# The high halves of the weights written by a converting DMA from GpSimd, instead of by GpSimd additions

## What is computed

```python
# first block
h = rmsnorm(x, pre_norm_g)
q, k, v, g_a, u_p, g_p = split(h @ w_in)                      # 1024 x 2304
a = banded_attention(q, k, v, rel_bias, attn_sink) * silu(g_a)
p = multiscale_pool(u_p, pool_w, pool_scale) * silu(g_p)
x = x + rmsnorm(concat([a, p]) @ w_out, post_norm_g)
# second block
h = rms_norm(x, norm1_g)
q, k, v, bg, cg, xc = split(h @ w_in_2)                       # 1024 x 6144
y_attn = chunked_relpos_attention(q, k, v, q_norm_g, k_norm_g, rel_bias) @ w_attn_proj
y_conv = gated_short_conv(bg, cg, xc, conv_w, conv_b) @ w_conv_proj
g_attn, g_conv = split(sigmoid(h @ w_gate + b_gate))
x = x + (g_attn * y_attn + g_conv * y_conv) @ w_out
h2 = rms_norm(x, norm2_g)
x = x + square(relu(h2 @ w_up)) @ w_down                      # 1024 x 4096 x 1024
```

## Time and profile before

| | us |
|---|---|
| median of 3 runs | 2715.04 (2714.69 to 2716.16) |
| the profiled execution, its own time | 2712.78 |
| its span in the profile | 2710.9 |
| PE busy | 2378.0 (88%) |
| PE weight loads busy | 2121.8 (78%) |
| DVE busy | 1203.3 (44%) |
| POOL busy | 926.5 (34%) |
| ACT busy | 677.1 (25%) |
| read from HBM, written | 160.83 MB, 60.82 MB |

### The profile page before, as it was taken

The page is one execution under the profiler, slowest core; times in us unless marked ns, Lnnn a source line. Parts: engine busy times, 40 slices in busy tenths (PEclk is TensorE's granted clock), DMA queues, the critical chain, the costliest instruction groups (busy, mean ns, idle before and its releaser), DMA issues. The chain is left out here.

```text
span 2710.9 us, 38552 instructions
## 1 busy us (share of the span) xinstructions
PE 2378.0 (88%) x14666; PEld 2121.8 (78%) x14666; DVE 1203.3 (44%) x2564; ACT 677.1 (25%) x1341; POOL 926.5 (34%) x736
## 2 busy tenths in 40 slices
PE   6237887378799969999999998999999999999999
PEld 6236766277799968888888876888979989889889
DVE  5006767636356626666666656133332122131121
ACT  3005545313200015555555512121211010010110
POOL 3031220234344422222222235444244444354352
PEclk9668997588999989999999999999989999999999
DMA  7833321221222232323333245222111111111112
GB/s 150 118 81 81 92 66 52 98 109 70 86 78 85 86 110 79 91 81 87 94 94 90 79 160 209 94 93 101 48 32 59 46 37 47 48 47 48 48 47 79
DMA packets 217453, 223.55 MB, mean 82 GB/s; under 512 B 81592, under 2 KB 185560, under 8 KB 217320
## 3 DMA queue, kind: packets, MB, share of 16 engines
q1 hardware_dynamic: 103384, 128.23, 16.4%
q10 hardware_dynamic: 113936, 93.44, 11.5%
HBM read 160.83 MB, written 60.82 MB: 82 GB/s over the span
## 5 line engine op out<-in xcount | busy, mean ns | idle before, releaser
L139 POOL TENSOR_TENSOR w_hi<-w_raw,zero 128x512 fp32r<-128x512 f32 x356 | 412.8, 1190 | 1589.9 <-PE ps L184 1298.7
L184 PE MATMUL ps<-a_hi,w_hi 128*128 128x512 f32 x1600 | 580.7, 409 | 20.7 <-DVE a_lo L374 9.9
L184 PE MATMUL ps<-a_lo,w_hi 128*128 128x512 f32 x1600 | 558.9, 395 | 5.8 <-issue 5.8
L184 PE MATMUL ps<-a_hi,w_lo 128*128 128x512 f32 x1600 | 559.3, 395 | 0.0
L184 PE MATMUL ps<-w_hi,a_hi 128*128 128x256 f32 x1472 | 424.8, 289 | 102.2 <-PEq L603 88.4
L144 POOL TENSOR_TENSOR w_lo<-w_raw,w_hi 128x512 fp32r<-128x512 f32 x356 | 471.9, 1357 | 7.0
L184 PE MATMUL ps<-w_lo,a_hi 128*128 128x256 f32 x1472 | 422.1, 287 | 0.0
L184 PE MATMUL ps<-w_hi,a_lo 128*128 128x256 f32 x1472 | 421.7, 286 | 0.0
L184 PEld LDWEIGHTS ps<-w_hi,a_hi 128*128 128x128 f32 x1472 | 288.9, 196 | 104.0 <-POOL w_lo L144 83.2
L184 PEld LDWEIGHTS ps<-a_hi,w_hi 128*128 128x128 f32 x1600 | 304.6, 191 | 75.9 <-issue 22.1
L184 PEld LDWEIGHTS ps<-a_hi,w_lo 128*128 128x128 f32 x1600 | 304.3, 190 | 67.5
(11 more groups left out here) (138 smaller groups left out, 2789.6 us busy)
## 6 DMA issues: line engine op xcount, KB each, us to landing
w_raw<-in_w_in_dram SPq DMA_DIRECT2D x33, 1024.0 KB, 5.2
feat_fm<-stage_a ACTq DMA_DIRECT2D x64, 256.0 KB, 2.0
w_raw<-in_w_up_dram SPq DMA_DIRECT2D x16, 1024.0 KB, 5.5
w_raw<-in_w_down_dram SPq DMA_DIRECT2D x16, 1024.0 KB, 5.1
qk_raw_a<-qkv_tm ACTq DMA_DIRECT2D x48, 256.0 KB, 3.8
conv_in<-feat_fm ACTq DMA_DIRECT2D x24, 512.0 KB, 5.5
qkv_tm<-stage_tm ACTq DMA_DIRECT2D x11, 1024.0 KB, 5.2
res<-in_x_dram SPq DMA_DIRECT2D x16, 512.0 KB, 6.0
```

What stands on the lines that cost most here:

```text
L139: hi = nc.gpsimd.tensor_tensor(w_hi[slot][:, k:k + 2, :], w_raw[:, k:k + 2, :], zero[:, 0:1].unsqueeze(2).to_broadcast([P, 2, CW]), ALU.add)
L184: last = nc.tensor.matmul(out_of(o), lhs, rhs(o), start=first and n == 0, stop=final and n == 2)
```

## The change

The four additions of zero that made the high half are gone. In their place POOL issues, as soon as the slot is free, one DMA of 1 MB that reads the chunk again from HBM and writes it into `w_hi`; source float32 and destination fp32r differ, so the DMA converts. Then POOL waits for both `raw_in` and `hi_done` (16 for each DMA now) and makes the low half with the same four subtractions as before. `w_raw` is still loaded by SP, in the same order. `split_weights` now needs the address of the chunk and so walks over `segs`; `phase_mlp` has the same edit by hand. PE, DVE, ACT and SP keep their instructions.

```diff
-        def pieces(slot, high_ready):
-
-            for k in range(0, KB, 2):
-                hi = nc.gpsimd.tensor_tensor(w_hi[slot][:, k:k + 2, :], w_raw[:, k:k + 2, :],
-                                             zero[:, 0:1].unsqueeze(2).to_broadcast([P, 2, CW]), ALU.add)
-            hi.then_inc(hi_done, 1)
-            high_ready()
+        def low_parts(slot):
+
             for k in range(0, KB, 2):
                 lo = nc.gpsimd.tensor_tensor(w_lo[slot][:, k:k + 2, :], w_raw[:, k:k + 2, :],
                                              w_hi[slot][:, k:k + 2, :].bitcast(F32), ALU.subtract)
             lo.then_inc(split_done, 1)
 
+        def rounded(w, row0, col):
+
+            return w[row0, :].rearrange("(k p) n -> p k n", p=P)[:, :, col]
+
...
-            def one(n, slot):
-                pool.wait_ge(raw_in, (n + 1) * 16)
+            def one(n, slot, w, row0, c):
                 if not (isinstance(n, int) and n - 2 < start):
                     pool.wait_ge(*used(n - (2 + start)))
-                pieces(slot, lambda: pool.wait_ge(hi_done, n + 1))
...
+                pool.dma_start(w_hi[slot][:, :, :], rounded(w, row0, c)).then_inc(hi_done, 16)
+                pool.wait_ge(raw_in, (n + 1) * 16)
+                pool.wait_ge(hi_done, (n + 1) * 16)
+                low_parts(slot)
...
                     def one(i, n, last=False):
                         slot = (start + n) % 2
-                        pool.wait_ge(raw_in, i * 128 + (start + n + 1) * 16)
...
-                        pieces(slot, lambda: pool.wait_ge(hi_done, i * 8 + (start + n + 1)))
+                        g, m = (i, n) if n < 8 else (i + 1, 0)
+                        if m < 4:
+                            src = rounded(io["w_up_2"], slice(0, D), bass.ds(g * D + m * CW, CW))
+                        else:
+                            src = rounded(io["w_down_2"], bass.ds(g * D, D), slice((m - 4) * CW, (m - 3) * CW))
+                        pool.dma_start(w_hi[slot][:, :, :], src).then_inc(hi_done, 16)
+                        pool.wait_ge(raw_in, i * 128 + (start + n + 1) * 16)
+                        pool.wait_ge(hi_done, i * 128 + (start + n + 1) * 16)
+                        low_parts(slot)
```

More of the change, by code:

```diff
@@ L146, in pieces @@
             lo.then_inc(split_done, 1)
+        def rounded(w, row0, col):
+            return w[row0, :].rearrange("(k p) n -> p k n", p=P)[:, :, col]
         def split_weights(pool, first, last, start, used, rolled=True):
-            def one(n, slot):
-                pool.wait_ge(raw_in, (n + 1) * 16)
+            def one(n, slot, w, row0, c):
                 if not (isinstance(n, int) and n - 2 < start):
                     pool.wait_ge(*used(n - (2 + start)))
-                pieces(slot, lambda: pool.wait_ge(hi_done, n + 1))
[L157 to L167, removed]
+                pool.dma_start(w_hi[slot][:, :, :], rounded(w, row0, c)).then_inc(hi_done, 16)
+                pool.wait_ge(raw_in, (n + 1) * 16)
+                pool.wait_ge(hi_done, (n + 1) * 16)
+                low_parts(slot)
+            for s0, s1, w, row0, col0 in segs:
+                lo, hi = max(s0, first), min(s1, last)
+                rows = slice(row0, row0 + D)
+                while lo < hi and lo < start + 2:
+                    one(lo, lo % 2, w, rows, bass.ds((lo - s0) * CW + col0, CW))
+                    lo += 1
+                pairs = (hi - lo) // 2
+                if pairs > 1 and rolled:
+                    with pool.Fori(0, pairs) as i:
+                        for q in range(2):
+                            one(i * 2 + (lo + q), (lo + q) % 2, w, rows,
+                                bass.ds(i * (2 * CW) + ((lo + q - s0) * CW + col0), CW))
+                    lo += 2 * pairs
+                for n in range(lo, hi):
+                    one(n, n % 2, w, rows, bass.ds((n - s0) * CW + col0, CW))
         def feed(block, start, count, used):
```

## The result

| | before | changed |
|---|---|---|
| median of the runs (4 each), us | 2714.86 | 2752.43 (2747.61 to 2760.60) |
| ratio, with its 95% interval | | 1.0141 (1.0111 to 1.0171) |
| the profiled execution, us | 2712.78 | 2747.84 |
| its span, us | 2710.9 | 2746.1 |

The change makes the kernel 1.4% slower. 2714 us with a range up to 2733 was forecast, so the range did not hold it. The profiled execution is at the lower end of the runs; what spreads the runs over 13 us stays open.

What follows compares the result with a forecast made beforehand. PE was taken as the bound (busy 88% of the span), with POOL waiting for it. Terms 0.7 - 4.0 + 1.0 + 2.0 - 0.5 = -0.8 us gave 2712.0 profiled, 2714 us as median; range 2704 to 2733.

Steps and rivals of the forecast that it cites:

- Steady chunks: nothing, as long as L is under about 16 us: MLP and attention chunks: POOL's waiting covers the new DMA, with 8.9 us to spare in the MLP and more in attentions.
- L: Time from POOL's issue of the 1 MB DMA to its landing, taken as 7 us; lower bound 5.2, 12 carried above.
- D: Starts of both attentions: the DMA delays the first head's load, 1.0 us each, +2.0 us, from 0 to +4.8.
- A: Chunk 2 in n1: 4.1 us of additions saved, stores and raw load slowed 4.8; +0.7 us, from -6 to +8.
- B: Attention a1: two PE waits for small DVE operations shrink once POOL's high half goes; -4.0 us, from -7.8 to 0.
- C: n2: low halves end later, before the first addition and at chunk 5; +1.0 us, from 0 to +11.
- E: Start of phase_branches: DVE's first `a_lo` row comes earlier with POOL quiet; -0.5 us, from -1.9 to +1.
- The rival of the slow DMA: Whole kernel: landing takes 12 us, giving +17 us, 2732; chance 0.24 for landings of 9 to 16 us, 0.05 above.
- its point of 15.9 us: MLP: landing time at which cover is gone (21.8 - 5.9); beyond it each microsecond costs about one per chunk.
- The rival of chunk 1 behind the stores: n1: chunk 1's DMA needs 20 us or more, PE stands there; cost 0 to 3 us, no chance of its own.
- What was named as a sign of error: PE waiting for `w_lo` in steady chunks, or PE's matmuls or DVE slowing beside 89 MB more traffic, would refute the forecast.
- The rule on VectorE and GpSimd's descriptors: DVE operations may hold up POOL's DMA, longest in the attentions where cover exceeds 15 us; under 1 us on the sum.

Runs made afterwards that it cites:

- only_a2: Kernel before, with the converting DMA in the second attention alone (16 chunks), all other chunks by additions: 2733.46 us, ratio 1.0071 to the kernel before.
- late_attn: Changed kernel, but in both attentions POOL issues the DMA some 9 us after the slot is free: 2731.51 us, ratio 1.0067 to the kernel before.
- starts_only: Kernel before, with the converting DMA only for the first chunk split in each of the two attentions: 2721.49 us, ratio 1.0028 to the kernel before.
- n1_only: Kernel before, with the converting DMA only for the three chunks of n1: 2716.27 us, ratio 1.0008 to the kernel before.
- chunk2_only: Kernel before, with the converting DMA only for chunk 2 of n1, issued while the long stores run: 2709.85 us, ratio 0.9985.
- best_of: Kernel before, with the converting DMA only in a1 from its second chunk, the 10 chunks of q, k, v, and phase_branches: 2710.91 us, ratio 0.9987.
- branch_tm: Kernel before, with the converting DMA only for the 10 chunks of q, k, v and the 8 of phase_branches: 2711.16 us, ratio 0.9988.

## Why the prediction was wrong

- **The step that failed: "Steady chunks: nothing, as long as L is under about 16 us".** The cover was worked out for POOL's own chain, raw load, high half, low half, and there it was right in a2 and in the MLP. What the new DMA does to other loads that are issued at the same instant was not asked for steady chunks. I had seen the collision at the starts of the attentions (D), and did not see that it comes back at every chunk, because head and chunk are both 8 steps long. The slack of 2.8 us could be read from the trace of before; but by my own bound for such a pair, 2.4 us, the load would still have come in time, so the size failed as well as the place. only_a2 gives 19.6 us for it with the start, late_attn takes it away.
- **D, the starts: right mechanism, size off.** 1.0 us each was taken, "the head's load is the smaller party". Measured 3.0 and 3.3 (starts_only). A load in 1024 rows of 256 bytes does not lose in proportion to its bytes; v went from 4.6 to 8.3 us while the 1 MB went from 5.7 to 8.0.
- **A, n1: +0.7 forecast, +3.4 in the changed kernel, +3.7 for the low half in n1_only.** The 4.1 us of additions did fall out of the path. The foreign traffic was priced well enough: in chunk2_only 1 MB delayed the raw load by 2.6 us (low half at 159.48; raw load at 156.92 before), where 2.1 was the rate. What failed is "I put its effect at 0" for chunk 0: it delays the stores by 5.4 us, of the 7.8 by which the raw load then came later.
- **B, a1: -4.0 forecast, -0.4 measured in best_of.** The range "from -7.8 to 0" held with its upper end. The second wait of the term went as forecast (3.9 us to 0.2 in five periods), the first did not (waits for `st_a` 15.9 us before, 16.2 in best_of), and the collision with the v load, which had no term here either, took 4.3 us back. The chunk period fell from 35.7 us to between 35.2 and 35.5 in the changed kernel, not to 34.9. DVE in a1 of the changed kernel, against the earlier trace rows:

```profile
256.26 0.16 DVE L1179 TENSOR_TENSOR st_a<-st_a,sink_a 128x1 f32<-128x1 f32 x1
...
257.86 0.35 DVE L1204 TENSOR_SCALAR prob_a<-prob_a,st_a 128x256 f32<-128x256 f32 x1
...
265.76 1.21 DVE L1204 TENSOR_SCALAR prob_a<-prob_a,st_a 128x384 f32<-128x384 f32 x1
```

  Line 1174 (now 1179) is back at 0.16 us and 1199 (1204) at 0.35 where the high half was, but the low half, which now begins 3.6 us later than it did, blocks another row for 1.21 instead of 0.42 us. That part of the cost has moved and not gone.
- **C, n2: +1.0 forecast, +4.0 in the changed kernel, +2.2 to +2.7 alone.** The place before the additions behaved as forecast: from slot to first addition 12.2 us against 11.3. The loss came from the block's end, where the term had 0.2 us, and in the changed kernel from its first chunk too, which had no term.
- **E, phase_branches: -0.5 forecast, -2.0 measured**, and -2.3 to -2.9 in four other kernels. The eight `a_lo` rows took 1491 ns at the mean instead of 1925: the low half came 5 us later (1684.04 in branch_tm, 1679.12 before), when about half of them were written. PE's waits for them fell from 9.9 to 8.2 us. The direction was right, the size too small.
- **No term at all: the convolution's block**, +4.5 and +7.0 us. The rival of the slow DMA held there among the steady chunks alone: L of 10 to 16 us, and its point of 15.9 us, worked out with a low half of 5.9 us, falls to 21.7 - 8.1 = 13.6 us with one of 8.1.
- **The rival of chunk 1 behind the stores came true, at no price that shows.** Its DMA landed 30 us after the issue, and the wait for POOL's low half in n1 that was named as its sign is there, ending at 62.66 us, the longest of its line in the whole span of the changed kernel:

```profile
PE ps L189 <- POOL w_lo L139: 27.3, 4, 20.1
```

  The wait at n1's end fell from 83.0 to 64.7 us, so chunk 2 covered it, as the prediction said.
- **The slow DMA as a whole** was rightly thought unlikely. Had its case been put as "slow where others load", it would have named n1, n2, both attentions and the convolution.
- **What was named as a sign of error** came true in part: PE waited for `w_lo` in steady chunks of one block, though PE and DVE did not slow down beside the traffic in the MLP (184 us of it hold 179.68 us of PE's work in place of 179.90, and 33.84 of DVE's in place of 39.00).
- The rule on VectorE and GpSimd's descriptors that was weighed (the Trainium skill, "SBUF — State Buffer", who interferes with whom) states that GpSimd can't write its descriptors while VectorE runs an operation that takes both ports. That would bear on POOL's own time for the issue: 0.91 us in the MLP. In a2 8 of 16 issues took 0.91 or 0.92 us and the others 1.03 to 1.16, as at 1201.49, where a 128x640 scaling of DVE (0.56 us) began 0.12 us behind it. Where the issue took 0.91 us (1087.76, 1164.64, 1238.54), the scaling began 0.3 us behind it and took 0.86 to 0.89 us itself. The trace agrees in sign, with a quarter of a microsecond on one engine or the other, under the 1 us that was allowed.

## What to carry to other kernels

A transfer that is hidden for its own reader is not free: before adding one, list which loads are issued in the same microseconds and what slack each of these has, landing against first use, and check whether two loops have the same period and so collide each time. A transfer with cover to spare is best issued into the gap (9 us later cost nothing in a2; at the end of a1 it was not free), and best not at all at a block's start beside its first loads. An edit that helps in some places and costs in others is worth placing chunk by chunk.

## What the runs showed of the hardware

- A load in 256-byte pieces beside a 1 MB DMA with 1 KB pieces took 8.3 us instead of 4.6, the 1 MB one 8.0 instead of 5.7.
- A converting DMA of 1 MB from GpSimd lands after 5.7 to 6.4 us in the MLP, little later than a plain one from SP (5.0 to 5.4), and beside the two long stores after 30 and 60 us. It makes a packet for each 1 KB, the plain one from GpSimd of the same bytes a quarter as many (2882 against 10976), and the two cost the kernel the same (2726.90 and 2727.12 us).
- When SP had issued 0.75 MB just before, ACT's instruction that issues a 256 KB load took 3.5 us at the median of 13 and 4.35 at most instead of 0.72 and 0.83, and ACT stood meanwhile. With GpSimd as the issuer of the same bytes it took 0.48 to 0.77.
- A 128x128 scaling on DVE took 2.27 us where POOL's additions ran, against 0.29 without them and 0.68 beside them in the kernel before, after a shift of 1 us in POOL's work; 38.4 us of PE's idle time then stood in 13 waits behind DVE.
